# Splitting the rows of four expert-weight transfers into 112, 8 and 8

## What is computed

```
hb = silu(xb @ w_gate[e]) * (xb @ w_up[e])      # w_gate, w_up: 2048 x 512 for each expert
y += (hb @ w_down[e]) * weight                  # w_down: 512 x 2048
```

## Time and profile before

| | |
|---|---|
| median of three runs | 1440.29 us |
| the profiled execution, its own time | 1437.99 us |
| its span, first to last instruction | 1436.2 us |
| TensorE (PE) busy | 1212.8 us, 84% of the span |
| VectorE / ScalarE busy | 32% / 18% |
| bytes moved by DMA | 479.30 MB |
| mean granted TensorE clock | 0.935 |

### The profile page before, as it was taken

One profiled execution on the slowest core, in us unless ns is written; L12 is line 12 of the kernel. 1 busy time (PEld: TensorE's weight loads), 2 busy tenths in 40 slices (PEclk: granted clock), 3 DMA queues, 4 the chain that ended last, 5 costly groups with the idle time before them and its releaser, 6 DMA issues.

```text
span 1436.2 us, 17426 instructions
## 1 busy us (share of the span) xinstructions
PE 1212.8 (84%) x7229; PEld 706.8 (49%) x7229; DVE 460.9 (32%) x953; ACT 253.2 (18%) x627; POOL 13.5 (1%) x82
## 2 busy tenths in 40 slices
PE   8999999999999999569789966769677695876976
PEld 7998989776558854124234413214242141422422
DVE  5399655473774541111110210111101111011123
ACT  2101210244610122002110101002010020100212
POOL 2000000000010000000000000000000000000000
PEclk9999999999999999879999988969989798897999
DMA  9946795413445799999999999999999999999996
GB/s 318 272 146 216 134 230 180 104 49 85 118 125 198 277 393 429 428 427 427 429 427 428 428 427 428 428 427 426 428 430 428 425 429 429 426 427 429 428 426 243
DMA packets 132352, 479.30 MB, mean 334 GB/s; under 512 B 47692, under 2 KB 105264, under 8 KB 106800
## 3 DMA queue, kind: packets, MB, share of 16 engines
q1 hardware_dynamic: 125808, 477.58, 85.6%
q10 hardware_dynamic: 6464, 0.58, 0.4%
HBM read 476.05 MB, written 2.10 MB: 333 GB/s over the span
## 4 chain that ended last, share of the span: by engine, by line
PE 52%; DMA 43%; DVE 2%; ACTq 2%; ACT 1%; issue 1%; SPq 0%; DVEq 0%
DMA ring<-in_expert_w_up_dram 34%; PE PS L1071 10%; PE PS L1388 10%; DMA spare<-in_expert_w_up_dram 6%; PE PS L1215 5%; PE PS L1063 5%; PE PS L1115 3%; PE PS L1375 3%; PE PS L1192 2%; DMA fin_g<-in_final_norm_g_dram 2%; PE PS L1555 2%; ACTq L1773 2%; PE PS L1366 1%; PE PS L1438 1%; PE PS L1167 1%; PE PS L1565 1%
## 5 line engine op out<-in xcount | busy, mean ns | idle before, releaser
L1388 PE MATMUL PS<-ring,XG 128*32 128x512 f32 x1296 | 229.0, 751 | 147.4 <-DMA ring<-in_expert_w_up_dram 105.8
L1388 PEld LDWEIGHTS PS<-ring,XG 128*32 128x32 f32 x1296 | 58.5, 134 | 278.6 <-issue 276.1
L2961 DVE TENSOR_TENSOR hTe<-PS,sg 128x128 f32<-128x128 f32 (+1 forms) x31 | 9.9, 319 | 354.7 <-ACT sg L2100 354.5
L2776 DVE TENSOR_TENSOR x<-PS,x 128x1024 f32<-128x1024 f32 x43 | 52.6, 1224 | 210.3 <-PE PS L1455 207.8
L2088 ACT ACTIVATE Hs<-PS 128x512 f32<-128x512 f32 x31 | 18.5, 597 | 487.2 <-PE PS L1388 376.3
L1375 PE MATMUL PS<-ring,XG 128*64 128x512 f32 x192 | 84.7, 594 | 15.3 <-DMA ring<-in_expert_w_up_dram 12.6
L1388 PE MATMUL PS<-spare,XG 128*32 128x512 f32 x208 | 67.5, 809 | 27.0 <-DMA ring<-in_expert_w_up_dram 27.0
L1455 PE MATMUL PS<-Y,SW 128*128 128x512 f32 (+2 forms) x176 | 89.0, 616 | 1.5 <-ACT ro L2198 1.5
L1377 PE MATMUL PS<-ring,XG 128*64 128x512 f32 x192 | 85.0, 595 | 0.0
L1063 PE MATMUL PS<-hT,ring 128*128 128x256 f32 x384 | 84.0, 379 | 0.0
L1366 PEld LDWEIGHTS PS<-sel,xn 128*128 128x128 f32 x640 | 75.3, 191 | 12.9 <-issue 12.7
(11 more groups left out here) (477 smaller groups left out, 1523.8 us busy)
## 6 DMA issues: line engine op xcount, KB each, us to landing
ring<-in_expert_w_up_dram SPq DMA_DIRECT2D x54, 2048.0 KB, 23.5
ring<-in_expert_w_gate_dram SPq DMA_DIRECT2D x54, 2048.0 KB, 26.5
ring<-in_expert_w_down_dram SPq DMA_DIRECT2D x51, 2048.0 KB, 26.6
ring<-in_w_in_dram SPq DMA_DIRECT2D x17, 2048.0 KB, 10.5
spare<-in_expert_w_gate_dram SPq DMA_DIRECT2D x9, 2048.0 KB, 26.8
spare<-in_expert_w_down_dram SPq DMA_DIRECT2D x9, 2048.0 KB, 26.6
spare<-in_expert_w_up_dram SPq DMA_DIRECT2D x8, 2048.0 KB, 23.4
ring<-in_w_in_dram SPq DMA_DIRECT2D x16, 512.0 KB, 7.1
```

The costliest lines, as they stand in the source:

```text
L1388: mm = pe.matmul(PS[r:r + 32, 0, :], XG[:, part, 4 * c + j, column:column + 32], weight_rows(slots[u], 4 * (c % 2) + j), start=(c == 0 and ...
L2776: dve.tensor_tensor(y, new, old, ALU.add).then_inc(sc_added, 1)
```

## The change

Four chunks are marked: chunk 0, a half of gate, of the experts at places 8, 14, 20 and 26 of the order. For these the loop issues three transfers in place of one: rows 0 to 111, rows 112 to 119, rows 120 to 127. Each adds 16 to the slot's semaphore, and `PLACED` counts the two that are added.

```diff
+UNEVEN = [CHUNKS * n for n in (8, 14, 20, 26)]
+UNEVEN_ROWS = [(0, 112), (112, 120), (120, 128)]
+
+
-PLACED = [16 * sum(1 + (h in IN_HALVES) for h in range(g + 1) if SLOT_OF[h] == SLOT_OF[g]) for g in range(E * CHUNKS)]
+PLACED = [16 * sum(1 + (h in IN_HALVES) + 2 * (h in UNEVEN) for h in range(g + 1) if SLOT_OF[h] == SLOT_OF[g]) for g in range(E * CHUNKS)]
...
                 for dst, src in chunk_parts(e, c, SLOT_OF[g]):
-                    sp.dma_start(dst, src).then_inc(e_loaded[SLOT_OF[g]], 16)
+                    for a, b in UNEVEN_ROWS if g in UNEVEN else [(0, P)]:
+                        sp.dma_start(dst[a:b, :], src[a:b, :]).then_inc(e_loaded[SLOT_OF[g]], 16)
```

## The result

The changed kernel takes 1488.8 us (median of 4 runs, 1486.92 to 1492.07) against 1440.66 us of the kernel before in the same job. The ratio is 1.0338, 95% interval 1.0325 to 1.0350: **48 us slower**. I had forecast slower, but 16 us, with a range up to 1471 us. The measured time lies 18 us above it.

A forecast was written before the change was run, and what follows sets the result against it. DMA engines' speed through 2 MB chunks was taken to bound the end. Pieces 19.7 us less a 4.9 us lead (14.8), plus 1.2 for the 112 rows: 16.0 us, forecast 1456.3 us against 1440.29, range 1437.5 to 1471 us.

The forecast's parts named there:

- What bounds the kernel, and that a late landing moves the end one for one: From 560 us on: DMA engines' speed through 2 MB chunks sets the end; 15 us follow the last landing, fin_g.
- The signs that the prediction named: Profile after: rate below 427 GB/s at uneven chunks, packets well over 0.617 us, longer up-weight waits, tail over 8 us.
- Issues and waits at nothing: SyncE's queue: eight more issues, 2.7 us in all, hidden by a 27.9 us backlog; TensorE waits for the latest landing.
- Destinations as the place of the cost: Writes into SBUF: output projection's 64-partition loads ran at about 220 GB/s, engines waiting for each other at the destination.
- The 112 rows: Large transfer of each marked chunk: engine and partitions may not fit one to one; 0.3 us each, 1.2 us for four.
- What one engine falls behind it never gets back: Steady chunk stream: engines always have several chunks queued and never run dry, so an engine's lag persists to the end.
- The pieces, 16 packet times in place of 8 on eight engines, 19.7 us: 8-row transfers: each piece 2.47 us on the same eight engines, plus turns with others; 4.94 us per chunk, 19.7 for four.
- The lead: Tail: if the piece-carrying eight are those early at the end, their lead pays the first 4.9 us, leaving 14.8 us.
- The early and the late eight of the earlier trace: Tail of the kernel before: eight engines are done 4.9 us or more before the last one.
- rival 1: Tail: pieces at full speed on early engines even the load; late eight finish 2.47 us sooner, 1437.8 us; chance 0.20.
- Rival 3: Pieces narrow to the end, 4.9 us each: 37.0 us for four chunks less 4.9, +32 us, 1472.4 us; chance 0.10.
- A slip in the range: Forecast case's low end, 12 us: 15 packet times, no 112-row loss, taken as 17.1 - 4.9 = 12.2.

The follow-up runs named there:

- e2: Kernel before, with the four marked chunks cut by columns (3584, 256, 256) into three transfers, all into 128 partitions: ratio 1.0014, +2 us.
- e4: Changed kernel's three transfers, each reading one and the same memory row for all its rows; against the kernel before: ratio 1.0308, +44 us.
- e1: Four marked chunks loaded as 112 and 16 rows, against the kernel before: ratio 1.0263, +38 us.
- e3: Four marked chunks loaded as two contiguous halves of 64 rows, against the kernel before: ratio 1.0236, +34 us.
- e9: Four marked chunks loaded as 96 and 32 rows, against the kernel before: ratio 1.0287, +41 us.
- f4: Four marked chunks loaded as four transfers of 32 neighbouring rows, against the kernel before: ratio 1.0228, +33 us.
- e10: Four marked chunks loaded as two transfers of every second row, 64 rows each, against the kernel before: ratio 1.0004.
- e6: Kernel before plus, behind each marked whole chunk, two extra half-size 8-row transfers, rows four apart in partitions 64 to 95: ratio 1.0047, +7 us.
- e6b: Kernel before plus, behind each marked whole chunk, two extra half-size 8-row transfers, rows four apart in partitions 0 to 31: ratio 1.0004, +0.6 us.
- f2: Two neighbouring chunks (place 14, chunks 0 and 1) each loaded in two 64-row halves, against the kernel before: ratio 1.0071, +10 us.
- f1: One chunk (place 14, chunk 0) loaded in two 64-row halves, against the kernel before: ratio 1.0059, +8.5 us.
- e7: Only one chunk loaded as 112, 8, 8 rows, against the kernel before: late (place 26) ratio 1.0082, +12 us; early (place 8) 1.0060, +8.7 us.
- e5: Kernel before plus, behind each marked whole chunk, two extra half-size 8-row transfers into partitions 112 to 127: ratio 1.0051, +7 us.

## Why the prediction was wrong

*What bounds the kernel, and that a late landing moves the end one for one*: right. The tail is the same 15 us, TensorE waits for nothing new. The signs that the prediction named came too: the rate drops, packets well over 0.617 us, longer waits for up weights, and more than 8 us between the first engine's end and the last one's.

*Issues and waits at nothing*: right; e2 shows two more transfers per chunk for +2 us (0.6 to 3.3), packets of 1 KB included.

*Destinations as the place of the cost*: right. The half rate of the 64-row loads carried over to 16 KB rows, and e4 puts it at the destination.

*The 112 rows, "between 0 and about one packet time per chunk, I take a half, 4 x 0.3 = 1.2 us"*: this is the step that failed. In the transfer of 112 neighbouring rows the packets take 1.2 us in place of 0.617, seven of them, on all 16 engines: 7 x 0.6 = 4.2 us per chunk where the sum had 0.3, and outside the 0 to 0.6 that it allowed. e1, e3, e9 and f4 lose 33 to 41 us with no transfer that few engines carry. I had taken the half rate of the 64-row loads as a matter of how many partitions a transfer reaches, and so saw narrowness in the pieces alone. e10 (64 rows that lie over all partitions, no loss) and e6 against e6b speak for another reading: two engines write partitions that one entry serves, and wait for each other there. ("Entry" is the prediction's word for a way into SBUF that several partitions share.) A transfer that covers nearly all partitions can have that as well. That the cost lies in which partitions are written is shown; the shared entry is the reading that fits, since the profile names neither the engine nor the partition of a packet.

*"What one engine falls behind it never gets back", and the cost ends with the chunk*: the first half holds, as the lags of the landings show, but the sum had no term for the whole chunks beside the split one, and this is the second step that failed. e3 loses 8.5 us per chunk where the sharing inside explains 4.9; f2 beside f1 says that this rest comes with the run of split chunks and not with each. The likeliest reading is that early engines are in the next chunk, writing their own partitions, while late ones still write into those from the split chunk. With a larger spread that lasts longer. The packets over 0.9 us in the four dips of the changed kernel are 182, 222, 288 and 289, of which at most 128 are the marked chunk's; in the early chunk alone 191, in the late one 274. That a dip grows with the spread (8, 11, 14, 15.5 us at 2.9, 4.3, 7.2, 10.2 us) fits this, and so do e7's medians, whose intervals overlap; the early one's own spread of 4.7 us fits it less well. It is not shown: no run changed the spread by itself.

*The pieces, 16 packet times in place of 8 on eight engines, 19.7 us*: too large, and on the wrong engines. Two pieces in place of 16 rows cost about 11 us, e5 at half size 7 us. The change's dip has 5 us at a third of the rate behind the half, and all 16 engines are busy in it (101.7% in 716 to 721 us): the pieces slow the others too.

*The lead, "the first 4.9 us are paid by their lead"*: wrong, as far as one profile shows. In e6b the two latest engines are among the eight that carry pieces, and the two earliest are not. The early and the late eight of the earlier trace rows are not the two groups that a piece of 8 rows makes, though six of the carriers are early ones. By the same fact rival 1 had no basis: even with no clash, the last engine would have had a packet more in each of the four chunks. e6b could not have shown a gain, since it takes no packet from the other eight.

*Rival 3* gave +32 us by pieces of 4.9 us. It came nearer in size and is false: at half size, in e5, its pieces would have lost 4 x 4.9 = 20 us, or 15 after the lead, and 7 us were measured.

*A slip in the range*: 15 packet times are 4 x 7 x 0.617 = 17.3 us more, not 17.1. It changes nothing.

The direction came out as forecast, but only in small part for the reason given: of the 48.7 us about 11 come from the pieces, the rest from the term put at 1.2 us and from the one that was missing.

The sum as it should have stood, an estimate for one marked chunk: 7 x 0.6 = 4.2 us for the 112 rows, a little under 3 us for the pieces (11 us over four), and the rest of what the dips cost, 1 to 8 us, for the whole chunks beside it, growing with the spread: 8 to 15.5 us. What remains open is which rows an engine takes in a transfer of fewer than 128: neither neighbouring shares nor the pattern of 128 rows scaled down (theory R) fits both e10 (no meeting) and f4 (packets twice as long). The profile does not name the engine of a packet.

## What to carry to other kernels

Where the DMA engines are the bound, cut a transfer by columns (e2, +2 us), or by every second row (e10, nothing), and not into blocks of neighbouring rows (+33 to +48 us). A halved rate at full engine share in some other load of the same kernel is the sign that engines wait for each other at the destination; before using it, ask which engine writes where, not how many rows there are. And one awkward transfer also slows the good ones beside it: in every dip looked at, more packets were slow than the split chunk has.

## What the runs showed of the hardware

- Blocks of neighbouring rows, whether 112, 96, 64 or 32, ran at half the rate (about 215 GB/s of 427), all 16 engines busy with packets of 1.2 us; 64 rows two apart ran at 428.
- A transfer of 8 rows has eight landings, one of 16, 32, 64, 96, 112 or 128 rows has 16. A transfer of 8 rows into other engines' partitions also slowed 61 packets of the whole chunks (e6).
- The engines' lags persist and grow with instruction code: in the kernel before, the packets of code on one queue, 16 KB each, are each followed in the next chunk's landings by one landing that is 1.5 us later than it was (all twelve between 560 and 900 us). The last landing of a chunk trails the first by 2.1 us at 560 us and by 7.7 us at 1388 us.
- The engines that carry a transfer of 8 rows include the two latest of the stream, and not the two earliest (the profile of e6b).
